# Matmuls of two sums in turn: gate and up tiles in the wide feed forwards, token tiles in the projections

## The reference

```
def swiglu_2(h, w_gate, w_up, w_down):
    return (jax.nn.silu(h @ w_gate) * (h @ w_up)) @ w_down
```

## Time and profile before

| | |
|---|---|
| median of 3 runs | 2593.58 us (2590.45 to 2596.62) |
| span of the profiled execution (its own time) | 2591.3 us |
| TensorE matmul busy | 2494.1 us, 96% |
| VectorE busy | 1335.6 us, 52% |
| ScalarE busy | 1035.0 us, 40% |
| DMA | 372.28 MB, mean 144 GB/s |

### The profile page before, as it was taken

How to read it: one execution, slowest core, us unless ns; L and a number is a source line. 1 busy time by engine, 2 the same in 40 slices (tenths; PEclk the granted TensorE clock), 3 DMA queues, 4 the chain that set the end, 5 groups by cost and what they waited for, 6 DMA issues and landing times. The chain is left out here.

```text
span 2591.3 us, 37219 instructions
## 1 busy us (share of the span) xinstructions
PE 2494.1 (96%) x15710; PEld 2161.8 (83%) x15710; DVE 1335.6 (52%) x2198; ACT 1035.0 (40%) x1660; POOL 0.2 (0%) x4
## 2 busy tenths in 40 slices
PE   7999999989999999999888999999999998988999
PEld 6998789978998888888567888888888887878999
DVE  6657454655554333456886433335333337846553
ACT  5534444444433223146562322213222226744443
POOL 0000000000000000000000000000000000000000
PEclk9999999999999999999998999999999999999999
DMA  8986733488862333335102333333333336502564
GB/s 307 306 266 215 244 122 99 139 311 303 313 227 87 94 96 97 98 114 187 58 1 66 90 98 98 98 98 90 98 98 97 95 93 171 186 18 66 175 183 147
DMA packets 146727, 372.28 MB, mean 144 GB/s; under 512 B 20330, under 2 KB 67074, under 8 KB 146562
## 3 DMA queue, kind: packets, MB, share of 16 engines
q1 hardware_dynamic: 146274, 369.59, 44.4%
q10 hardware_dynamic: 288, 0.31, 0.1%
HBM read 368.71 MB, written 1.15 MB: 143 GB/s over the span
## 5 line engine op out<-in xcount | busy, mean ns | idle before, releaser
L298 DVE TENSOR_TENSOR weights_lo<-weights_raw,weights_hi 128x1024 fp32r<-128x1024 f32 (+2 forms) x547 | 657.4, 1212 | 485.0 <-ACT weights_hi L292 482.9
L350 PE MATMUL psum<-normed_hi,weights_hi 128*128 128x256 f32 (+2 forms) x2664 | 884.1, 332 | 22.6 <-DVE normed_lo L629 6.5
L350 PE MATMUL psum<-normed_lo,weights_hi 128*128 128x256 f32 (+2 forms) x2664 | 869.9, 327 | 0.0
L350 PE MATMUL psum<-normed_hi,weights_lo 128*128 128x256 f32 (+2 forms) x2664 | 869.3, 326 | 0.0
L292 ACT CAST weights_hi<-weights_raw 128x1024 fp32r<-128x1024 f32 (+2 forms) x547 | 562.7, 1035 | 374.1 <-DMA weights_raw<-in_w_down 254.3
L350 PEld LDWEIGHTS psum<-normed_hi,weights_hi 128*128 128x128 f32 (+1 forms) x2664 | 512.0, 192 | 86.0 <-issue 35.1
L350 PEld LDWEIGHTS psum<-normed_lo,weights_hi 128*128 128x128 f32 (+1 forms) x2664 | 513.2, 193 | 41.5 <-issue 1.2
L350 PEld LDWEIGHTS psum<-normed_hi,weights_lo 128*128 128x128 f32 (+1 forms) x2664 | 512.9, 193 | 40.7
L350 PE MATMUL psum<-hidden_hi,weights_hi 128*128 128x512 f32 (+1 forms) x594 | 217.6, 366 | 0.0
L350 PE MATMUL psum<-hidden_hi,weights_lo 128*128 128x512 f32 (+1 forms) x594 | 217.1, 365 | 0.0
L350 PE MATMUL psum<-hidden_lo,weights_hi 128*128 128x512 f32 (+1 forms) x594 | 217.0, 365 | 0.0
(11 more groups left out here) (264 smaller groups left out, 2724.1 us busy)
## 6 DMA issues: line engine op xcount, KB each, us to landing
weights_raw<-in_w_gu SPq DMA_DIRECT2D x220, 512.0 KB, 3.6
weights_raw<-in_w_down SPq DMA_DIRECT2D x110, 512.0 KB, 3.6
arena<-in_w_mod SPq DMA_DIRECT2D x72, 512.0 KB, 7.1
weights_raw<-in_w_x SPq DMA_DIRECT2D x24, 512.0 KB, 7.4
resid<-in_w_mod SPq DMA_DIRECT2D x24, 512.0 KB, 7.6
normed_raw<-in_w_mod SPq DMA_DIRECT2D x24, 512.0 KB, 6.9
under_normed_hi<-in_w_mod SPq DMA_DIRECT2D x24, 512.0 KB, 7.2
weights_raw<-in_w_qk SPq DMA_DIRECT2D x24, 512.0 KB, 3.7
```

Source lines behind the costliest of these rows:

```text
L298: ve.tensor_tensor(w_lo[:, c % RING, a], w_raw[:, c % RING, a], w_hi[:, c % RING, a].bitcast(F32), ALU.subtract).then_inc(lo_ready, 1)
L350: last = te.matmul(out, a, b, start=start and n == 0, stop=stop and n == 2)
```

## The change

**Feed forwards of 512 tokens.** From chunk 4 on, TensorE does nothing in the step of an even chunk (gate), and in the step of the odd one (up) it does both: for each k tile, high by high for gate, then for up, high by low for both, low by high for both. It waits for the low part of the second chunk and for both banks ahead of the first matmul, and counts `used` up by two at the end. ScalarE and VectorE read gate and up sums together in the odd step (`ended`). These stages get a fourth bank, and `groups` now picks for each sum the bank whose last sum lies longest back.

**Projections.** `LinearT.tensor` now takes the two token tiles in turn for each of the three matmuls, and waits for both banks ahead of a block's first matmul.

```
             def wait_bank(self, pe, g):
-                if self.group + g >= BANKS:
-                    pe.wait_ge(*bank_free[self.group + g - BANKS])
+                if self.bank_before[g] is not None:
+                    pe.wait_ge(*bank_free[self.bank_before[g]])
...
             def tensor(self, pe, i):
                 c, (b, part) = self.first + i, divmod(i, self.per)
                 pe.wait_ge(lo_ready, c + 1)
-                for n, t in enumerate(self.tiles):
-                    g = b * len(self.tiles) + n
-                    if part == 0:
-                        self.wait_bank(pe, g)
-                    for j in range(self.each):
-                        k = part * self.each + j
...
+                first = b * len(self.tiles)
+                if part == 0:
+                    for n in range(len(self.tiles)):
+                        self.wait_bank(pe, first + n)
+                for j in range(self.each):
+                    k, w = part * self.each + j, slice(j * self.width, (j + 1) * self.width)
+                    if b == 0 and self.ready:
+                        pe.wait_ge(*self.ready(k))
+                    hi, lo = w_hi[:, c % RING, w], w_lo[:, c % RING, w]
+                    for n, (weights, which) in enumerate(((hi, 0), (hi, 1), (lo, 0))):
+                        for m, t in enumerate(self.tiles):
+                            last = te.matmul(psum[:, self.bank(first + m), 0:self.width],
...
             ready = True
+            def in_pair(self, chunk):
+
+                return self.paired and chunk > HALVED
...
+            def tensor(self, pe, i):
+                chunk, tokens, _, _ = self.pass_of(i)
+                if not self.in_pair(chunk):
+                    super().tensor(pe, i)
+                    return
+                if chunk % 2 == 0:
+                    return
+                c = self.first + chunk
+                pe.wait_ge(lo_ready, c + 1)
+                for b in (chunk - 1, chunk):
+                    self.wait_bank(pe, self.sum_at[b, None])
+                for k in range(KD):
+                    tile = slice(k * P, (k + 1) * P)
+                    for n, (weights, x) in enumerate(((w_hi, 0), (w_hi, 1), (w_lo, 0))):
+                        for b in (chunk - 1, chunk):
+                            last = te.matmul(self.sums(b), weights[:, (self.first + b) % RING, tile],
+                                             self.x[x][:, k, tokens],
+                                             start=k == 0 and n == 0, stop=k == KD - 1 and n == 2)
+                last.then_inc(used, 2)
```

More of the change, by code:

```diff
@@ L299, in split_lo @@
                                  ALU.subtract).then_inc(lo_ready, 1)
-        bank_free = []
+        bank_free, bank_last = [], {}
         TABLES_LN_EXP = 6
@@ L316, in place, with groups @@
                 chunk_at.extend((weights, k, self.size) for k in range(self.n))
-            def groups(self, evacs):
-                self.group = len(bank_free)
+            def groups(self, evacs, banks=range(BANKS)):
+                self.group, self.bank_of, self.bank_before = len(bank_free), [], []
                 for name in evacs:
+                    bank = min(banks, key=lambda b: bank_last.get(b, b - 8))
+                    self.bank_of.append(bank)
+                    self.bank_before.append(bank_last.get(bank))
+                    bank_last[bank] = len(bank_free)
                     bank_free.append((evac_act if name == "evac_act" else evac_dve, take(name, 1) + 1))
             def bank(self, g):
-                return (self.group + g) % BANKS
+                return self.bank_of[g]
             def wait_bank(self, pe, g):
-                if self.group + g >= BANKS:
-                    pe.wait_ge(*bank_free[self.group + g - BANKS])
+                if self.bank_before[g] is not None:
+                    pe.wait_ge(*bank_free[self.bank_before[g]])
             def sync(self, sp, i):
@@ L358, in __init__ @@
             def __init__(self, weights, k_tiles, blocks, x, a, dest, func=ACT.Copy, scale=None, evacs=None,
-                         evac=None, head=None, tail=None):
+                         evac=None, head=None, tail=None, banks=range(BANKS)):
                 self.place(weights)
@@ L372, in __init__ @@
                 self.sum_at = {(b, half.start if half else None): g for g, (b, half) in enumerate(sums)}
-                self.groups([evac] * len(sums) if evac else evacs or ["evac_act"] * blocks)
+                self.groups([evac] * len(sums) if evac else evacs or ["evac_act"] * blocks, banks)
                 self.n = len(self.passes)
@@ L460, in tensor @@
                 pe.wait_ge(lo_ready, c + 1)
-                for n, t in enumerate(self.tiles):
-                    g = b * len(self.tiles) + n
-                    if part == 0:
-                        self.wait_bank(pe, g)
-                    for j in range(self.each):
-                        k = part * self.each + j
[L467 to L472, removed]
+                first = b * len(self.tiles)
[10 more added lines that the diff above has]
+                            last = te.matmul(psum[:, self.bank(first + m), 0:self.width],
+                                             self.x[which][:, k, t * P:(t + 1) * P], weights,
+                                             start=k == 0 and n == 0, stop=k == self.k_tiles - 1 and n == 2)
                 last.then_inc(used, 1)
@@ L642, in __init__ @@
             def __init__(self, weights, tiles, a, pair, norms):
+                self.paired = len(norms) > 1
                 super().__init__(weights, KD, 2 * tiles, normed, a, None, evacs=["evac_act", "evac_dve"] * tiles,
-                                 head=[norm.a for norm in norms] if len(norms) > 1 else None)
+                                 head=[norm.a for norm in norms] if self.paired else None,
+                                 banks=range(BANKS + 1) if self.paired else range(BANKS))
                 self.pair, self.norms = pair, norms
@@ L651, in build, with ended @@
             ready = True
+            def in_pair(self, chunk):
+                return self.paired and chunk > HALVED
+            def ended(self, chunk):
+                if self.in_pair(chunk):
+                    return [chunk - 1, chunk] if chunk % 2 else []
+                return super().ended(chunk)
+            def tensor(self, pe, i):
[17 more added lines that the diff above has]
+                last.then_inc(used, 2)
             def ready_for(self, tokens, k):
@@ L2113, in build @@
                  joined(down, norms, beside(steps_of(*ab_main), side)))
-        first_needs = [bank_free[-1 - n] for n in range(BANKS)] + [turns.done(9)]
+        first_needs = [bank_free[g] for b, g in sorted(bank_last.items()) if b < BANKS] + [turns.done(9)]
         units = []
@@ L2202, in build @@
                                     [heads.done(need), (kr_spread, 1)], dest[0:MQ, h:h + 2, :]) for h in range(0, 8, 2)]
-        first_needs = [bank_free[-1 - n] for n in range(BANKS)] + [(bias_in, grid_load.landed)]
+        first_needs = [bank_free[g] for b, g in sorted(bank_last.items()) if b < BANKS] + [(bias_in, grid_load.landed)]
         base = counts["turns"]
```

## The result

The changed kernel takes 2608.7 us (median of 4 runs, 2606.41 to 2612.17) against 2595.02 us (4 runs, 2590.45 to 2596.62) for the kernel before. The ratio is 1.0063 with an interval of 1.0044 to 1.0083, that is 16 us, between 11 and 22. The forecast was 18 us for the profiled execution and 2611.6 us for the median. The profiled executions are 14.2 us apart, 2605.5 against 2591.3.

The account below looks back on a forecast made before the run. TensorE's queue, busy 96% of 2591.3 us, was taken as the bound. Matmul rate 0, bank wait +18 and pairs 0 made 2609.3 us, or 2611.6 us for the median; forecast range 2604 to 2620.

Parts of the forecast that it names:

- The matmul rate: Feed forwards and projections: alternating banks saves none of each matmul's fixed 13.3 ns, so 0 us; far end 54 us gained.
- rival A: Feed forwards and projections: alternating banks does remove the fixed part, giving 2557.6 us, faster by 1.4%; chance 0.15.
- rival B: Matmul rate: only part of the gain comes, or only in one stage; 2596 down to 2588 us; chance 0.07.
- The bank wait: Projections: waiting for both banks first leaves ScalarE's read uncovered at 23 places, 18 us slower, between 12 and 25.
- the 1 us that it took off: Projections: deduction for delay taken up where TensorE later waits for VectorE or ScalarE anyway.
- rival D: Projections: the new waits are absorbed by TensorE's other waits, so nothing happens; given no chance of its own.
- The 3.3 us that the forecast counted there: Second projection stage: TensorE's existing waits for ScalarE, counted among 4.9 us of waits that might take up delay.
- The two places where ScalarE comes late: Projections: TensorE already waits there; six matmuls now come after the wait, costing 0.80 us more and 1.36 us more.
- the term of 18 us: Projections: the forecast's total loss from waiting for both banks ahead of a block's first matmul, between 12 and 25 us.
- The pairs: Wide feed forwards: pair starts find weights and banks ready with over 5 us to spare, so 0 us.
- Rival C: Wide feed forwards: the second chunk's low part comes late, say 0.5 us per pair, 30 us more, 2642 us; chance 0.03.

Follow-up runs that it names:

- the waits first: Kernel before, matmul order kept and no pairs; only the second bank's wait moved ahead of a block's first projection matmul: 2613.55 us, ratio 1.0092.
- one matmul of cover: Changed kernel without pairs, projections in the new order, second bank's wait only ahead of the second matmul: 2602.06 us, ratio 1.0052 against the kernel before.

## Why the prediction was right

**The matmul rate.** The step went from two bank changes in the kernel before that saved nothing to no saving in steady alternation. The three stretches and the run of the pairs alone bear it out. The objection that a single change may not show what steady alternation does (rival A, 0.15) was fair to hold open and did not come true; rival B fell with it.

**The bank wait.** The count of places was exact: in the trace after, TensorE stands still ahead of a block's first matmul at 23 places (20 in the row above, one more under another tile's name, and two that the view puts down to weights). Sized by kind: at a straight 512-column place 1.02 us against 0.95 forecast with the restart. Behind a transpose step most show 0.45 us idle, against 0.49 to 0.72.

One term of each place was too small. From the end of ScalarE's read to TensorE's start the forecast took 0.05 us, from the earlier trace rows, where the wait stands in the middle of a chunk. At the blocks' starts after the change it is 0.14 us, as above, or 0.25, as here:

```profile
1172.29 0.38 ACT L487 ACTIVATE arena<-psum 128x256 f32<-128x256 f32 x1 [3.93 <-PE psum L476]
```

```profile
1172.92 0.70 PE L476 MATMUL psum<-weights_hi,normed_hi 128*128 128x512 f32 x2 [0.68 <-ACT arena L487]
```

Over 21 places that makes an estimated 3 us, which the forecast did not have. Against it more was taken up by other waits than the 1 us that it took off: TensorE stood 3.1 us for its transposes' inputs in the two stages before and stands 0.5 us after (of rival D, which had all of the loss absorbed, that much came true). The 3.3 us that the forecast counted there end at 2284.22, behind the last projection matmul, and are still 3.3 us after.

The two places where ScalarE comes late went apart from the forecast. By it TensorE would stand 1.47 + 0.80 = 2.27 us at the first and 0.92 + 1.36 = 2.28 at the second. It stands 0.70 us at the first, and the second now shows the longest wait:

```profile
2192.22 0.70 ACT L487 ACTIVATE arena<-psum 128x288 f32<-128x288 f32 x2
...
2192.88 0.70 PE L476 MATMUL psum<-weights_hi,normed_hi 128*128 128x512 f32 x2 [4.38 <-ACT arena L487]
```

That is 4.38 us against 0.92 at that place before. ScalarE had to wait there for a load of `w_dq` first, and that waiting varies: the longest wait is 3.1 us in the run of the projections alone, 4.1 with the waits first and 5.5 with half the stationary columns, and the runs with four banks have it under `weights_lo` and `cq_t_lo`. The two places together are only 0.5 us above the forecast, but behind the long stop the clock fell, which no term of the forecast had:

```profile
2193.60:2197.00 3.40, 3.40 (x9) 2.63 (x9) 2.24 (x9) 1.66 (x4) 0.00 (x0) 0.50 0.91 208
```

```profile
2194.13 1.05 PE L476 MATMUL psum<-weights_lo,normed_hi 128*128 128x512 f32 x2
2194.98 1.05 PE L476 MATMUL psum<-weights_hi,normed_hi 128*128 128x512 f32 x2
```

The matmuls come every 0.43 us instead of 0.227, at 1.2 GHz; over 3.4 us that loses an estimated 1.7 us. The second stage grew by as much above its forecast, 12.7 us instead of 11. A long stop alone doesn't decide it: in the run of the projections alone the same place stands 3.1 us and the clock from 2180 to 2200 us is 1.00. The first stage grew by 6.1 us where 7 were forecast; before, 3.4 us of it ran at 1.2 GHz behind a stop of 2.1 us for weights, after, none did, which gives back another 1.7 us.

So the term of 18 us fits the 18.8 us by which the stages grew, and the mechanism is right, but part of that fit is luck. A release time that was too small, by some 3 us in all, and other waits that took up 1.6 us more than assumed cancel in part, and the two clock losses cancel each other. The forecast had no term for the clock at all, which moved the profiled difference by 5 us. The projections measured alone, 21 us, are above the term and inside its bounds of 12 to 25.

**The pairs.** Costed at nothing, with over 5 us to spare. ScalarE's rows in the first wide feed forward after:

```profile
1006.12 0.60 ACT L707 ACTIVATE arena<-psum 128x512 f32<-128x512 f32 x1 [6.17 <-PE psum L685]
1007.48 0.62 ACT L710 CAST hidden_hi<-arena 128x512 fp32r<-128x512 f32 x1 [0.76 <-DVE arena L721]
1008.00 1.04 ACT L292 CAST weights_hi<-weights_raw 128x1024 fp32r<-128x1024 f32 x1
1009.78 1.05 ACT L292 CAST weights_hi<-weights_raw 128x1024 fp32r<-128x1024 f32 x1 [0.73 <-DMA weights_raw<-in_w_down]
1017.00 0.60 ACT L707 ACTIVATE arena<-psum 128x512 f32<-128x512 f32 x1 [6.17 <-PE psum L685]
```

The second split waits 0.73 us for its load, which the forecast did not have, and ScalarE is then idle for 6.17 us until the pair ends. With VectorE's 1.23 us behind it the weights are ready at 1012.1, 4.7 us ahead of the next start at 1016.8, so the slack is a little under the forecast's. Rival C (a stall per pair) did not occur, nor did a third wait instruction cost anything.

**What the Trainium skill's rules came to.** The place of the waits decided, and with a fourth bank the loss went from 16 us to 3, with an interval from 0 to 6. This agrees with the Trainium skill ("Perfetto Trace Analysis", section "Matmuls"), which asks for rotation through banks so that the reading of one overlaps the next matmuls. The Trainium skill's rule of columns / 2.4 GHz and 2.5 ns for back-to-back matmuls ("TensorE: Matmul & The Clock Gate", section "Wait — 56ns, not 53.3ns?") does not hold for matmuls with a weight load each in this kernel: 226.7 ns with fp32r and 225 with strided bf16, against an estimated 216 by the rule.

## What to carry to other kernels

Before an order of instructions is changed for a rate, look for a place where the old program already does the new thing once: here a bank change in the middle of a chunk said in three rows what 2880 matmuls then confirmed. When two sums are made in turn, both of their banks are needed at the start, so a rotation that was deep enough for sums one after the other is one bank short; either give it as many banks as two rounds of sums need, or leave work ahead of the second wait that lasts as long as a read. A moved wait costs the time until its release less the work that still stands ahead of it, and here 0.09 to 0.20 us more where it joined other waits at a block's start. Compare the granted clock before two profiled spans are subtracted: here it hid 5 us of 19.

## What the runs showed of the hardware

At a granted clock of 1.00 an fp32r matmul with its own weight load costs its columns at 2.4 GHz and 13.3 ns: 0.120 us for 256 columns, 0.2267 for 512 and 0.133 for 288, whichever bank it goes to and, at 512, whether its weights are new or repeated. At 1.2 GHz the fixed part doesn't show: the 512-column matmuls from 2194.13 on take 0.85 us for two, 0.425 each, where 512 columns at 1.2 GHz are 0.427 us and 13.3 ns more would make 0.440. Loading half the stationary columns made a matmul slower, not faster (230 ns against 226.7 over the 960 paired matmuls of the stretch above), which I had not expected and cannot explain.

From the end of ScalarE's read to TensorE's next matmul it is 0.05 us where the bank's wait stands ahead of a later matmul of the block (the earlier trace rows and the run with one matmul of cover), and 0.14 or 0.25 us where it stands at the block's start with other waits. The second matmul after such a stop comes some 0.1 us late.
